# The first layer's row projection by pieces of its contraction, with input and row weights loaded in eight pieces by two queues

## The reference

```python
def layer_step(x, pos, lp, attn, ...):
    cols = x @ lp['w_in']                      # the input projection
    q, k, v, qi, ki, wi = ...                  # its first 932 columns: attention and its indexer
    y_a = attn(q, k, v, qi, ki, wi)
    y_b = rwkv7_mix(cols[..., B_START:B_END], ...)
    y_c = gated_short_conv(cols[..., C_START:C_END], ...)
    y_d = rglru_block(cols[..., D_START:D_END], ...)
    mix = concatenate([y_a, y_b, y_c, y_d]) @ lp['w_out']
    x = layer_norm(DEEPNORM_ALPHA * x + mix, ...)
    x = layer_norm(DEEPNORM_ALPHA * x + moe(x, ...), ...)
    return x, ...
```

## Time and profile before

| | |
|---|---|
| median of 3 runs | 1359.83 us (1358.13 to 1360.35) |
| profiled execution, its own time | 1366.04 us |
| its span, first to last instruction | 1364.4 us |
| instructions | 24557 |
| mean granted TensorE clock over the span | 0.908 of full speed |

### The profile page before, as it was taken

One profiled execution on the slowest core, in us unless ns is written; L12 is line 12 of the kernel. 1 busy time (PEld: TensorE's weight loads), 2 busy tenths in 40 slices (PEclk: granted clock), 3 DMA queues, 4 the chain that ended last, 5 costly groups with the idle time before them and its releaser, 6 DMA issues.

```text
span 1364.4 us, 24557 instructions
## 1 busy us (share of the span) xinstructions
PE 1148.9 (84%) x9786; PEld 699.0 (51%) x9786; DVE 649.8 (48%) x1353; ACT 329.4 (24%) x774; POOL 160.2 (12%) x225
## 2 busy tenths in 40 slices
PE   4989999997789829999499799999878991999940
PEld 2466878894354513333146667789735451333310
DVE  0035699687724430111463358988764434111128
ACT  1044224120532102111133342323034210111110
POOL 0050003502200020000200100061050002000020
PEclk9997999898799859999899889999889995999985
DMA  7079211002862376997720212110085518699832
GB/s 279 9 292 408 80 62 31 21 5 66 261 235 109 163 299 248 416 426 285 259 99 21 81 32 71 54 32 7 3 254 201 215 69 333 228 399 423 328 138 105
DMA packets 66468, 240.37 MB, mean 176 GB/s; under 512 B 8530, under 2 KB 29170, under 8 KB 56818
## 3 DMA queue, kind: packets, MB, share of 16 engines
q1 hardware_dynamic: 47872, 172.97, 33.7%
q0 software_dynamic: 14592, 52.10, 10.5%
q10 hardware_dynamic: 3890, 13.72, 2.5%
HBM read 190.21 MB, written 50.78 MB: 177 GB/s over the span
## 4 chain that ended last, share of the span: by engine, by line
PE 73%; DVE 10%; ACT 4%; DMA 3%; issue 3%; DVEq 2%; SPq 2%; POOL 1%; POOLq 0%; ACTq 0%
PE ps L748 14%; PE ps L1287 12%; PE ps L881 11%; PE ps L1244 8%; PE ps L728 8%; PE ps L1302 6%; SPq L482 2%; PE ps L1274 2%; PE ps L1116 1%; PE ps L807 1%; ACT arena L1380 1%; DMA arena<-in_wa 1%; DVE arena L1925 1%; DVE arena L2285 1%; POOL rows_in L659 1%
## 5 line engine op out<-in xcount | busy, mean ns | idle before, releaser
L1380 ACT ACTIVATE arena<-ps 128x512 f32<-128x512 f32 (+14 forms) x342 | 142.6, 454 | 653.6 <-PE ps L748 158.6
L748 PE MATMUL ps<-arena 128*128 128x272 f32 x1088 | 262.2, 401 | 0.0
L748 PEld LDWEIGHTS ps<-arena 128*128 128x128 f32 x1088 | 209.6, 194 | 51.0 <-issue 5.5
L1287 PE MATMUL ps<-arena 128*32 128x512 f32 x1536 | 169.7, 592 | 4.8 <-ACT arena L1380 4.8
L881 PE MATMUL ps<-arena 64*64 64x64 f32 (+3 forms) x4016 | 155.5, 238 | 14.1 <-DVE arena L2142 10.3
L881 PEld LDWEIGHTS ps<-arena 64*64 64x64 f32 x4016 | 141.0, 139 | 27.7 <-issue 16.2
L728 PE MATMUL ps<-arena 128*128 128x512 f32 (+1 forms) x256 | 106.7, 578 | 22.0 <-DMA arena<-in_wa 18.5
L1244 PE MATMUL ps<-arena 128*128 128x512 f32 x256 | 114.1, 601 | 0.0
L1287 PEld LDWEIGHTS ps<-arena 128*32 128x32 f32 x1536 | 51.2, 109 | 117.0 <-issue 117.0
L1302 PE MATMUL ps<-arena 128*32 128x512 f32 x768 | 87.4, 595 | 3.3 <-DVE arena L2600 2.0
L728 PEld LDWEIGHTS ps<-arena 128*128 128x128 f32 x256 | 50.0, 198 | 74.6 <-issue 74.5
(11 more groups left out here) (346 smaller groups left out, 1304.0 us busy)
## 6 DMA issues: line engine op xcount, KB each, us to landing
arena<-in_w_gu SPq DMA_DIRECT2D x32, 2048.0 KB, 13.8
arena<-in_w_dn SPq DMA_DIRECT2D x32, 1024.0 KB, 14.2
arena<-in_wf SPq DMA_DIRECT2D x34, 512.0 KB, 3.6
rows_in<-arena POOLq DMA_DIRECT2D x12, 1024.0 KB, 24.2
arena<-rows_in SPq DMA_DIRECT2D x24, 512.0 KB, 13.8
rows_out<-arena ACTq DMA_DIRECT2D x24, 512.0 KB, 8.7
arena<-in_cache_v POOLq DMA_DIRECT2D x64, 128.0 KB, 5.7
arena<-in_cache_k SPq DMA_DIRECT2D x64, 128.0 KB, 5.5
```

The source lines that it names most:

```text
L748: mm = pe.matmul(ps[:, 2 + 2 * h + n % 2, 0:HALF], m.wf[n % 3][:, c, :], m.xT[:, c, h * HALF:h * HALF + HALF], start=c == 0, stop=c == KC - 1)
L1287: mm = pe.matmul(ps[q, 3 + k, :], m.xgT[:, c, q], m.w_gu[HOME[i]][:, c, :], start=c == 0, stop=c == KC - 1, skip_group_check=True)
L1380: return act.activation(out, in_, ACT.Copy)
```

## The change

In the first layer the row projection goes chunk by chunk of the contraction: for each of the eight chunks, TensorE waits for that chunk of the input and of the row weights, and runs the eight groups' matmuls for it, each group into a bank of its own. All eight groups end in the last chunk. ScalarE copies group k out of bank k. The sample rows wait for the first copy only, and behind them TensorE waits for all eight. SyncE loads the input in eight pieces of one chunk, ScalarE's queue the row weights in eight pieces of one chunk (all 932 columns), ahead of its drains and constants. Both count on one semaphore for each chunk. The second layer keeps its projection and its loads.

```diff
 PER_LAYER = dict(
-    params_in=16, wa0_in=16, wa1_in=16, wf0_in=96, wf1_in=96, wf2_in=80, ln_in=64,
+    params_in=16, wf0_in=96, wf1_in=96, wf2_in=80, ln_in=64,
...
-ONCE = ("x_out", "const_in", "x_in", "x_copied", "zeroed", "zeros_out")
+FIRST = tuple(f"first{c}_in" for c in range(KC))
+ONCE = ("wa0_in", "wa1_in", *FIRST, "x_out", "const_in", "x_copied", "zeroed", "zeros_out")
...
 def sync_program(sp, s, m, din, dout):
     pages = m.pages
-    sp.dma_start(m.xT, din["xT"]).then_inc(s["x_in"], 16)
+    for c in range(KC):
+        sp.dma_start(m.xT[:, c, :], din["xT"][:, c, :]).then_inc(s[FIRST[c]], 16)
...
-    row_weights(0)
+    sp.dma_start(m.params, layer_of(din["params"], 0)).then_inc(s["params_in"], 16)
...
     def row_projection(l):
 
-        for h, (a, w) in enumerate(((0, 512), (512, ACOLS - 512))):
-            pe.wait_ge((s["wa0_in"], s["wa1_in"])[h], nth(l, f"wa{h}_in", 16))
-            for i in range(NT):
-                row_tile_half(l, NT * h + i, i, a, w)
-        sample_rows(l)
+        for c in range(KC):
+            pe.wait_ge(s[FIRST[c]], 32)
+            for k in range(2 * NT):
+                a, w = ((0, 512), (512, ACOLS - 512))[k // NT]
+                mm = pe.matmul(ps[:, k, 0:w], m.xT[:, c, row_tile(k % NT)], m.wa[:, c, a:a + w],
+                               start=c == 0, stop=c == KC - 1, skip_group_check=True)
+                if c == KC - 1:
+                    mm.then_inc(s["rows_mm"], 1)
+        sample_rows(l, 1)
+        pe.wait_ge(s["rows_copied"], nth(l, "rows_copied", 2 * NT))
...
         def half(i, h):
-            pe.wait_ge((s["wa0_in"], s["wa1_in"])[h], nth(l, f"wa{h}_in", 16))
+            pe.wait_ge((s["wa0_in"], s["wa1_in"])[h], 16 * l)
...
         pe.wait_ge(s["xt_copied"], nth(l, "xt_copied", 0))
-        sample_rows(l)
+        sample_rows(l, 2 * NT - 1)
...
-    def sample_rows(l):
-
-        pe.wait_ge(s["rows_copied"], nth(l, "rows_copied", 2 * NT - 1))
+    def sample_rows(l, copied):
+
+        pe.wait_ge(s["rows_copied"], nth(l, "rows_copied", copied))
...
     pe.drain().then_inc(s["mix_mm"], 1)
-    pe.wait_ge(s["x_in"], 16)
     for l in range(DEPTH):
...
             for k in range(2 * NT):
-                row_half(l, k, *divmod(k, NT))
+                row_half(l, k, *divmod(k, NT), k)
...
-    def row_half(l, k, h, i):
+    def row_half(l, k, h, i, bank):
 
         a, w = ((0, 512), (512, ACOLS - 512))[h]
         act.wait_ge(s["rows_mm"], nth(l, "rows_mm", k + 1))
-        copy(m.A[:, i, a:a + w], ps[:, k % 2, 0:w]).then_inc(s["rows_copied"], 1)
+        copy(m.A[:, i, a:a + w], ps[:, bank, 0:w]).then_inc(s["rows_copied"], 1)
...
+    for c in range(KC):
+        act.dma_start(m.wa[:, c, :], layer_of(din["wa"], 0)[:, c, :]).then_inc(s[FIRST[c]], 16)
     for name in ("xt_copied", "xgt_copied", "y_copied_a", "y0_stored", "y1_stored"):
         act.drain().then_inc(s[name], 1)
     act.dma_start(m.consts, din["consts"]).then_inc(s["const_in"], 16)
```

More of the change, by code:

```diff
@@ L1462, in rows_behind_norm @@
         deviation(l - 1, 5, 2, 2)
-        row_half(l, 0, 0, 0)
+        row_half(l, 0, 0, 0, 0)
         columns_of_x(l - 1, 5, 1, 1)
         deviation(l - 1, 5, 3, 3)
-        row_half(l, 1, 1, 0)
+        row_half(l, 1, 1, 0, 1)
         deviation(l - 1, 5, 4, 4)
@@ L1469, in rows_behind_norm @@
         for i in range(1, NT):
-            row_half(l, 2 * i, 0, i)
+            row_half(l, 2 * i, 0, i, 0)
             columns_of_x(l - 1, 5, i + 1, i + 1)
-            row_half(l, 2 * i + 1, 1, i)
+            row_half(l, 2 * i + 1, 1, i, 1)
     def columns(l, *chunks):
```

## The result

The changed kernel takes 1346.04 us (median of 5 runs, 1343.73 to 1351.06), the kernel before 1359.83 us in the same comparison (median of 5 runs, 1358.13 to 1366.36). The ratio is 0.9906, with a 95% interval of 0.9884 to 0.9927: 12.8 us less, between 9.9 and 15.8 (the two medians lie 13.8 us apart). The profiled execution took 1349.45 us with a span of 1347.8 us, 16.6 us less than the span before.

The account below looks back on a forecast made before the run. The start was taken as bound by TensorE's first load, then by TensorE itself. First pass from 18.51 to 5.8 us gives -12.7 us, all else nothing: 1359.83 to 1347.1 us, range 1344.0 to 1351.5 us.

Parts of the forecast that it names:

- The first wait: Start of the row projection: TensorE waits for 0.756 MB only, first pass at 5.8 instead of 18.51 us, gain 12.7 us.
- The upper end: First pass at 8.0 us: ScalarE's queue gets its first packet only after 5 us, 6.9 us plus 1.1 us lag.
- The 128 passes: Row projection on TensorE: still 52.99 us, slow first passes included; waits for a free bank go away, winning nothing.
- Sum: Whole kernel: 12.7 us less, span 1364.4 to 1351.7 us, median 1359.83 to 1347.1 us.
- Later pieces: Seven pieces after the first: 1.9 us transfer each against 6.6 us of TensorE work, cost nothing; one failure 2 us.
- The rule on transfer size: First pair's loads: batching to at least 1 MiB; at some 240 GB/s 1.3 us longer, gain 11.4 us.
- Constants and cache loads: Loads behind the weights: constants near 26 us, cache loads issued to about 62 us, 7 us left, cost nothing.
- Copies: End of projection: ScalarE keeps up, last copy ends 0.6 us after the last pass, hidden behind 3.29 us of sample rows.
- The rival of the banks: Row projection: changing bank each matmul keeps passes at 0.85 us, projection 99.8 us, kernel 1394 us; chance 0.04.
- Out of order: Start: all pieces come in together, first pass at 17 to 18 us, no change, 1359 us; chance 0.04.
- Given back later: Behind the projection: a wait, most likely for SyncE's cache loads, eats half the gain, 1353.5 us; chance 0.03.

Follow-up runs that it names:

- the second profile: The changed kernel run again unchanged, on another chip, against the kernel before on that chip: 1345.09 us, ratio 0.9869.

## Why the prediction was right

It said 1347.1 us, between 1344.0 and 1351.5; the median is 1346.04 us. The mechanism held; that the number came within 1.1 us is in part luck, since the start gave 1.4 us more than the sum had, the runs of one kernel spread over 7 us, and on the other chip the gain was 17.9 us. By its steps:

- **The first wait.** Said: first pass at 5.8 us, ends 4.4 and 8.0. Measured: 5.39 us, and 5.19 us in the second profile. The form of the sum held: 0.756 MB had moved by 4.5 us in the profile after, and the first pair was in at 5.35 us, a lag of 0.9 us against the 1.1 said. (The terms as given, 4.4, 1.1 and 0.14 us, add up to 5.6 and not to 5.8.) The upper end did not occur. It rested on ScalarE's first packet after 5 us; with SyncE's small pieces the packets came in the third microsecond. In the run with the order alone, with the large loads of before, they came after 5 us again (none in the first 5 us, 16 in the sixth microsecond), while in the run with one queue, with the same constants first on ScalarE's queue but the small pieces on SyncE's, the first came in the third microsecond. So the late start belongs to what stands on SyncE's queue.
- **The 128 passes.** Said: 52.99 us, seven slow passes. Measured: 52.01 us, four to five slow passes. This is 1.0 us that the sum did not have; how many passes are slow varied from profile to profile (the projection took 52.01 and 52.30 us in the two profiles of one program).
- **Sum.** 12.7 us said; 14.1 us at the start of the feature columns in the profile, 0.4 us from the first pass and 1.0 us from the slow ones. By the ratio it is 12.8 us, between the medians 13.8 us.
- **Later pieces.** Said: nothing. No gap in the 128 passes, from two queues or from one.
- **The rule on transfer size**, "DMA: Bandwidth & Descriptors" of the Trainium skill, section "Bandwidth" (at least 1 MiB at a time). An estimate from its table, which is for transfers issued by GpSimd, put the first pass 1.3 us later. Measured against it: queued one behind the other, the pieces of 272 and 466 KB, alone on both queues, moved 384 to 426 GB/s in every microsecond from 3 to 17 us, as much as the long loads before, and the first pass came 0.4 us earlier than said, not later.
- **Constants and cache loads.** Said: constants near 26 us, cache loads to 62 us, fourth feature chunk at 69.7 us, 7 us left. Measured: in by 26.0, then 61.5, 68.3 and 6.7 us. How late the constants could come was not tried.
- **Copies.** Said: ScalarE keeps up, last copy 0.6 us after the last pass, hidden by the sample rows. Measured: so.
- **The rival of the banks**, and the rule of the Trainium skill in "TensorE: Matmul & The Clock Gate", section "A second HAM failure mode: psum-queue depth-cycling". The passes stand 0.43 and 0.35 us apart through eight banks from 8.9 us to the end of the projection, so the clock did not fall in it. This trace does not bear the rule out for passes that follow one another without a gap.
- **Out of order.** The first pair landed first. **Given back later.** Not seen.

## What to carry to other kernels

Where a kernel starts with one large product, look at what the first instruction waits for, not at what it reads: cut the loads along the loop that runs outermost, and put that loop on the dimension in which every piece feeds much work. Here neither cut nor order was worth anything alone, and one queue did as well as two once the constants were held back; what mattered beside them was that nothing else of size moved until the first piece was in. When two profiles are compared far behind a change, compare the starts of the same work stretch by stretch, since here the distance went from 14 to 25 us and back to 17 in stretches in which the clock was low in only one of the two; two profiles of one and the same program stood 4 us apart by then.

## What was not expected

The prediction did not have the first two of these; the runs' own expectations did. Loads on another queue took most of the bandwidth: in the run with one queue the constants moved 0.37 MB in the fifth microsecond, the pieces that TensorE waited for 0.07 MB, and the first pass came 2.9 us later than with the constants held back (7.93 against 5.08 us). And passes on zeros raised the clock as real ones do: with four of them ahead of the projection one slow pass was left of four or five. No forecast had that the first packet on ScalarE's queue would come in the third microsecond once SyncE's queue held small pieces, instead of after 5 us.
